# The second half of an output product in two rounds, and an expert weight load that waits on the first of them

## The reference, cut to what matters

```
for l in range(DEPTH):                       # DEPTH = 2
    m = hybrid_mixer(h, ...)                 # ends in  y @ w_o
    h = layer_norm(ALPHA * h + m, ln1)       # "ln1"
    f = grouped_moe(h, w_router, ..., w_gate[l], w_up[l], w_down[l])
    h = layer_norm(ALPHA * h + f, ln2)
...
y = gates[0]*(o_diff @ w_br[0]) + gates[1]*(o_dsa @ w_br[1]) + gates[2]*(o_fox @ w_br[2])
return y @ w_o                               # 512x1024 @ 1024x1024: the output product
...
h = silu(xb @ w_gate[e]) * (xb @ w_up[e]);  return h @ w_down[e]   # one expert
```

## Time and profile before

| | us |
|---|---|
| median of 3 runs | 2340.98 (2340.57 to 2341.06) |
| the profiled execution | 2343.16 |
| its span | 2341.5 |
| TensorE busy | 2048.9 (88%) |
| VectorE busy | 935.6 (40%) |
| ScalarE busy | 656.8 (28%) |
| GpSimd busy | 194.6 (8%) |

### The profile page before, as it was taken

One profiled execution on the slowest core, in us unless ns is written; L12 is line 12 of the kernel. 1 busy time (PEld: TensorE's weight loads), 2 busy tenths in 40 slices (PEclk: granted clock), 3 DMA queues, 4 the chain that ended last, 5 costly groups with the idle time before them and its releaser, 6 DMA issues.

```text
span 2341.5 us, 29179 instructions
## 1 busy us (share of the span) xinstructions
PE 2048.9 (88%) x9720; PEld 1185.9 (51%) x9728; DVE 935.6 (40%) x1817; ACT 656.8 (28%) x1361; POOL 194.6 (8%) x233
## 2 busy tenths in 40 slices
PE   4999999999989988788679999989999799887882
PEld 3776676577653332222257657757767333232220
DVE  5764745444561111111268566445446411110114
ACT  3444355354310100000143435445451111000000
POOL 0000001000011111111100000010000111111111
PEclk9999999999989999999879999999999899999996
DMA  5221221222479999999832113213234999999994
GB/s 174 88 89 37 72 74 71 72 72 73 198 293 407 425 425 426 425 426 425 349 114 84 62 37 108 72 37 108 73 114 174 380 425 424 425 425 426 426 425 197
DMA packets 96160, 536.18 MB, mean 229 GB/s; under 512 B 15984, under 2 KB 18800, under 8 KB 72448
## 3 DMA queue, kind: packets, MB, share of 16 engines
q1 hardware_dynamic: 83712, 511.06, 53.9%
q0 software_dynamic: 12288, 23.11, 2.6%
HBM read 528.87 MB, written 23.07 MB: 236 GB/s over the span
## 4 chain that ended last, share of the span: by engine, by line
PE 70%; DVE 9%; DMA 8%; issue 7%; ACT 2%; another core or an unknown queue 1%; POOL 1%; SPq 1%; DVEq 0%; ACTq 0%; POOLq 0%
PE ps L980 16%; PE ps L696 10%; PE ps L698 10%; PE ps L697 10%; PE ps L996 8%; PE ps L882 5%; DMA scr<-in_w_up 4%; PE ps L798 2%; DMA spare<-in_w_up 2%; PE ps L849 2%; PE ps L820 2%; PE ps L972 1%; DMA scr<-h_rows,scr 1%; DVE small L1530 1%
## 5 line engine op out<-in xcount | busy, mean ns | idle before, releaser
L1886 DVE COPY scr<-ps 128x512 f32<-128x512 f32 x66 | 45.6, 692 | 770.9 <-PE ps L972 770.9
L696 PE MATMUL ps<-hT_lo,w_hi 128*128 128x512 f32 (+1 forms) x832 | 339.1, 408 | 15.5 <-DVE w_lo L1392 7.4
L698 PE MATMUL ps<-hT_hi,w_hi 128*128 128x512 f32 (+1 forms) x832 | 327.5, 394 | 0.0
L697 PE MATMUL ps<-hT_hi,w_lo 128*128 128x512 f32 (+1 forms) x832 | 326.6, 393 | 0.0
L1110 ACT ACTIVATE scr<-ps 128x512 f32<-128x512 f32 (+3 forms) x296 | 129.8, 440 | 399.2 <-PE ps L996 305.9
L1130 ACT ACTIVATE w_hi<-ring 128x1024 fp32r<-128x1024 f32 x124 | 130.5, 1053 | 292.9 <-PE ps L698 231.0
L1392 DVE TENSOR_TENSOR w_lo<-ring,w_hi 128x1024 fp32r<-128x1024 f32 x124 | 150.7, 1216 | 132.5 <-ACT w_hi L1130 129.1
L696 PEld LDWEIGHTS ps<-hT_lo,w_hi 128*128 128x128 f32 (+1 forms) x832 | 157.1, 189 | 54.4 <-issue 8.3
L1332 ACT ACTIVATE scr<-ps 64x512 f32<-64x512 f32 x64 | 37.7, 589 | 523.7 <-PE ps L981 523.7
L698 PEld LDWEIGHTS ps<-hT_hi,w_hi 128*128 128x128 f32 (+1 forms) x832 | 156.9, 189 | 35.7
L882 PE MATMUL ps<-scr,ring 128*128 128x512 f32 x384 | 171.7, 609 | 3.4 <-ACT scr L1110 3.4
(11 more groups left out here) (245 smaller groups left out, 3212.3 us busy)
## 6 DMA issues: line engine op xcount, KB each, us to landing
ring<-in_w_down SPq DMA_DIRECT2D x32, 2048.0 KB, 48.3
ring<-in_w_in SPq DMA_DIRECT2D x30, 2048.0 KB, 7.6
xslot<-in_w_up SPq DMA_DIRECT2D x18, 2048.0 KB, 46.1
wslot<-in_w_gate SPq DMA_DIRECT2D x16, 2048.0 KB
ring<-in_w_gate SPq DMA_DIRECT2D x16, 2048.0 KB, 44.4
ring<-in_w_up SPq DMA_DIRECT2D x16, 2048.0 KB, 48.5
scr<-in_w_down SPq DMA_DIRECT2D x16, 2048.0 KB
scr<-in_w_up SPq DMA_DIRECT2D x14, 2048.0 KB
```

The source lines that it names most:

```text
L696: mm(out, a[0], b[1], start=first, stop=False)
L697: mm(out, a[1], b[0], start=False, stop=False)
L698: return mm(out, a[0], b[0], start=False, stop=last)
```

## The change

The first half of the output product is as before. The second half is done in two rounds. Round one runs over all four tiles with only the low parts of `y`, 8 matmuls each. After its last matmul a new signal, `low_used`, ticks. Round two runs over the four tiles with the two products of `y_hi`, 16 matmuls each, and marks the bank full after each tile. The transposes keep their places behind tiles 2 and 3. SyncE's wait for slot 3 (piece 6), where `y_lo` lies, is now on `low_used` instead of on `("m", 3, 1)`.

```
@@ SyncE
                         elif s == 1:
                             multiplied(("m", NT - 1, 0))
+                        elif s == MRING:
+                            sp.wait_ge(low_used.sem, low_used.at("m", l))
+                            alone(sp)
                         elif s == H_SLOT:
@@ TensorE
-                    for half in range(2):
-                        for t in range(NT):
-                            free(4 + t, l)
-                            for k in range(KD):
-                                if t == 0:
-
-                                    pe.wait_ge(wo_ready.sem, wo_ready.at((half, k), l))
-                                    alone(pe)
...
-                                ins = product(t, half, k)
-                            filled(ins, 4 + t, ("m", t, half))
-                            if half and t >= 2:
-                                transpose_tile("ln1", t - 2, l)
+                    for t in range(NT):
+                        free(4 + t, l)
+                        for k in range(KD):
...
+                            ins = product(t, 0, k)
+                        filled(ins, 4 + t, ("m", t, 0))
+                    for t in range(NT):
+                        free(4 + t, l)
+                        for k in range(KD):
+                            if t == 0:
+
+                                pe.wait_ge(wo_ready.sem, wo_ready.at((1, k), l))
+                                alone(pe)
+                            ins = mm(bank[4 + t].t, y_lo[:, k, tok(t)], wo_hi(1, k), start=(k == 0), stop=False)
+                    ins.then_inc(low_used.sem, low_used.tick("m"))
+                    for t in range(NT):
+                        for k in range(KD):
+                            mm(bank[4 + t].t, y_hi[:, k, tok(t)], wo_lo(1, k), start=False, stop=False)
+                            ins = mm(bank[4 + t].t, y_hi[:, k, tok(t)], wo_hi(1, k), start=False, stop=(k == KD - 1))
+                        filled(ins, 4 + t, ("m", t, 1))
+                        if t >= 2:
+                            transpose_tile("ln1", t - 2, l)
```

More of the change, by code:

```diff
@@ L346, in trunk @@
         wo_ready = signal("wo_ready")
+        low_used = signal("low_used")
         aff_ready = signal("aff_ready")
@@ L889, in product @@
                                              (wo_hi(half, k), wo_lo(half, k)), k == 0, k == KD - 1)
-                    for half in range(2):
-                        for t in range(NT):
-                            free(4 + t, l)
-                            for k in range(KD):
-                                if t == 0:
-                                    pe.wait_ge(wo_ready.sem, wo_ready.at((half, k), l))
-                                    alone(pe)
-                                if t == 0 and half == 0:
-                                    pe.wait_ge(y_ready.sem, y_ready.at(("y", k), l))
-                                    alone(pe)
-                                ins = product(t, half, k)
-                            filled(ins, 4 + t, ("m", t, half))
-                            if half and t >= 2:
-                                transpose_tile("ln1", t - 2, l)
+                    for t in range(NT):
+                        free(4 + t, l)
+                        for k in range(KD):
+                            if t == 0:
+                                pe.wait_ge(wo_ready.sem, wo_ready.at((0, k), l))
+                                alone(pe)
+                                pe.wait_ge(y_ready.sem, y_ready.at(("y", k), l))
+                                alone(pe)
+                            ins = product(t, 0, k)
+                        filled(ins, 4 + t, ("m", t, 0))
```

## The result

The changed kernel took 2350.15 us, the median of 6 runs (2347.53 to 2357.32), beside 2340.64 us for the kernel before. The ratio is 1.0041, with a 95% interval of 1.0030 to 1.0053: **slower by 9.5 us** (7 to 12). Forecast were +5.7 us. All runs of both kernels made in this study, 20 of the changed one and 88 of the one before, have medians of 2349.08 and 2341.17 us. So the cost is about **7.9 us**. That lies near the lower end of the first measurement's interval; the two later series of the changed kernel alone gave +7.1 and +7.2 us.

The account below looks back on a forecast made before the run. Bound by the chain leading to expert 0, not by the weight stream. Per layer 2.6 + 1.6 - 0.3 = 3.9 us; two layers 7.8 less 2.1 back: +5.7 us, 2346.7 us; range -0.6 to +8.3 us (2340.4 to 2349.3).

Parts of the forecast that it names:

- the norm queue: VectorE's layer norm after the second half: tiles arrive faster than its 5.04 us each, router product 2.6 us late per layer.
- Given back: Expert stage: earlier pieces 14 and 15 remove stream dips, returning 1.4 us in the first layer and 0.7 in the second.
- Piece 6 and the dry stream: SyncE's weight stream: piece 6 out at about 651.3 us, DMA dry from about 697 until piece 12; no gain.
- The clock: TensorE's 2.6 us gap before tile 2's transposes halves the clock around router product and sum: +1.6 us per layer.
- The gather: Expert 0's first gather: issued at 690.4 us, 0.3 us shorter per layer, its length hardly following the DMA backlog.
- The third rival: First gather short once the DMA backlog is small, 3.5 us less per layer: -1.3 us in all, the same; chance 0.10.
- the two refunds: Dips before piece 14 in the expert stage vanish: 1.4 us back in the first layer, 0.7 in the second.
- the clock's bound: Most the low clock could cost at the router product and the sum behind it: 2.3 us instead of 1.6.

Follow-up runs that it names:

- load_real: Kernel before in its old order, early load added; second half's low-`y` product replaced by repeating the low-weights product: 2341.72 us beside 2341.12, ratio 1.0001.
- order_only: Changed kernel, but the load into the low parts' buffer waits again for the second half's last product: 2350.64 us, ratio 1.0044 to the kernel before.
- gap_filled: Changed kernel plus three useless matmuls between the transposes of tiles 1 and 2: 2348.69 us, ratio 1.0032; repeated 2345.29 us, 1.0021.
- delay4: Kernel before plus five useless matmuls in front of the router's product, nothing else: 2352.90 us, ratio 1.0052.
- whole2: Changed kernel with tiles 0 and 1 of the second half kept whole, only tiles 2 and 3 in two rounds: 2340.69 us beside 2341.05, ratio 0.9999.
- before_b: Kernel before, unchanged, measured against itself and profiled again: 2342.14 us, ratio 0.9999.

## Why the prediction was wrong

The direction, the norm queue and the fall of the clock were right. The step that failed is **"Given back"**: 2.1 us were to return, and the stretches show 0.5 us, which is less than their scatter. By the prediction's own steps:

- **Piece 6 and the dry stream.** Forecast 7.6 us after the end of the first half; 7.60. DMA was forecast dry from 697, which is 693.5 on this trace's clock; it is at 123 GB/s from 694 and at 20 from 695. That the early load is worth nothing is shown best by load_real, which has the load without gain or cost; order_only has the cost without it. The rule of the Trainium skill (Perfetto Trace Analysis, section Optimization Strategy), by which mixing stages with different busy engines may improve performance, gave nothing here; two kernels fill that idle time and both keep their time.
- **The norm queue.** Forecast: first tile 11.08 us after the end of the first half, one tile each 5.04 us, a gap of 2.6 us. Measured: 11.18, 5.0 and 2.45. The selection without the clock's part is 2.65 us late (gap_filled). Right.
- **The clock.** Forecast 2.8 us for the router's product and 0.3 for the sum. Measured 2.79 in four layers of the three profiles, 2.65 and 2.58 in the other two, and the sum unchanged at 0.83 in five of the six. The prediction held that nothing would bring the clock back before the filler products; in the profile shown it is at 1.00 again from 672 to 674 us, ahead of the fillers. In the sixth layer, and in one of order_only's two, the low clock caught the transposes and the sum too and cost 1.3 to 1.4 us more. So the term is 1.4 us in most layers and 2.7 to 2.8 in some; 1.6 lies between.
- **The gather.** Issued 46.58 us after the end of the first half, forecast 46.7. Its length of 6.82 us is 0.15 under before's 6.97; 0.3 were taken. With it piece 12 is 3.88 us late, against a forecast of 3.9. The third rival had the gather short once the backlog is small. That came true for the next gathers, which were issued at 697.2 and 698.5 us into idle DMA and landed in 2.7 and 2.9 us; the first one had DMA still at some 400 GB/s beside it until 694 us.

The gather and its length stand in the chain that ended last, in the changed kernel:

```profile
686.77 6.82 DMA scr<-h_rows,scr
```

- **Given back: this is the step that failed.** The prediction let 2.1 us return, by this chain: the wait for the second gather vanishes, so TensorE comes to expert 1 sooner after expert 0, so piece 14 goes out before the stream runs low, and a dip that is gone is time won. The first link is right: the gather falls into idle DMA, and the wait of 0.95 us for its rows is gone. The second one hardly held in the first layer. TensorE's first product of expert 1 stood behind VectorE's copy of the gathered rows, and that copy stands in VectorE's queue behind the hidden values of expert 0. Of the changed kernel, VectorE's and TensorE's timelines:

```profile
703.06 0.69 DVE L1916 TENSOR_TENSOR scr<-scr,ps 64x512 f32<-64x512 f32 x1 [4.84 <-ACT scr L1348]
703.78 0.69 DVE L1902 COPY scr<-ps 128x512 f32<-128x512 f32 x1
```

```profile
704.81 0.64 PE L996 MATMUL ps<-wslot,scr 128*64 128x512 f32 x1 [1.81 <-DVE scr L1902]
```

And of the kernel before:

```profile
702.67 0.69 DVE L1900 TENSOR_TENSOR scr<-scr,ps 64x512 f32<-64x512 f32 x1 [4.84 <-ACT scr L1332]
703.62 0.69 DVE L1886 COPY scr<-ps 128x512 f32<-128x512 f32 x1 [0.26 <-PE ps L972]
```

The copy's own wait of 0.26 us is all that the faster gather could save. Piece 14 follows piece 12 after 11.27 us instead of 11.51 (713.84 - 702.57, against 713.68 - 702.17), and the stream still dips. The window of the kernel before beside the 307 GB/s of the changed one:

```profile
713.00:717.00 4.00, 3.27 (x21) 1.47 (x20) 1.72 (x3) 0.59 (x1) 0.00 (x0) 1.00 0.80 266
```

By the prediction's own measure the dip was worth 4 x (425 - 266) / 425 = 1.5 us and is worth 1.1 us now. A part of the 11.27 us is the clock. Behind the 1.81 us of idle time it fell in the first layer of the changed kernel's three profiles, and held in order_only, which has the same idle time; the second matmul of expert 1's gate product in the changed kernel, then in order_only, 0.80 and 0.43 us ahead of the next of its line:

```profile
705.28 1.01 PE L996 MATMUL ps<-wslot,scr 128*64 128x512 f32 x1
```

```profile
704.50 0.59 PE L993 MATMUL ps<-wslot,scr 128*64 128x512 f32 x1
```

Where it held, in seven of the 13 profiles, piece 14 followed piece 12 after 9.58 or 9.59 us. And there the last link can be tested, that an earlier piece 14 is time won. It is not borne out: from piece 12 to the last store of the first layer these seven take 447.6 to 449.5 us, and the six with 11.27 to 11.51 us take 447.6 to 448.4. The lead of 1.7 us is still there at piece 32 and gone at piece 52, which goes out 166.8 to 167.8 us behind piece 12 in the seven and 166.9 to 167.4 in the six. In the second layer of the changed kernel piece 14 did follow sooner, after 9.58 us instead of 10.23, and nothing came back. What takes the lead away stays open.

Behind the selection the layers take 476.48 us in the mean of the changed kernel's three profiles and 477.24 before in the first layer (0.8 us given back, less than the scatter), and 478.00 against 477.73 in the second (nothing). delay4 gives back nothing either.

So the sum is 4.0 + 4.5 us to the selection (8.5, with the toss of the clock in the second layer), less 0.5 behind it: 8.0 us, and 7.9 us is what 20 and 88 runs say. With no refund the prediction's own terms give 7.8 us. That this comes so near is in part luck, since the second layer's 4.5 us hold one toss of the clock. No step shows the 1.6 us between 7.9 and the +9.5 us of the first measurement. The spread of a median of six runs can hold them, but this is argued and not shown: the three traced executions of the changed kernel are the fastest or second fastest of their series, and what the slower ones lose was not traced. +7.9 us lies inside the range and +9.5 us lies 0.85 us above its upper end. That end allowed for one of the two refunds lost, no gain at the gather and the clock's bound, and took nothing for the spread of a six run median, although two stages hang on a clock that falls in some executions and not in others.

## What to carry to other kernels

Before a buffer is freed early, ask what the next load behind it waits for. If that is a computed event, the early load only moves the idle time of the stream to another place. Regrouping products so that results come late and close together costs where the engine behind them works in order and needs longer per tile than the new distance; half of the tiles left as they were (whole2) kept the early load at no cost. A saving behind a delay counts only if every wait on the path of the next event is followed through, the in-order queue of the engine that releases it included. And a load that goes out earlier is a gain only if its lead is still there at the end of the stage.

## What the hardware showed that was not expected

- The same idle time does not always have the same effect on TensorE's clock. Behind 1.98 us at 106 to 108 us the granted clock was 0.57 over 4 us in one execution and 1.00 in another of one program. Behind 2.45 us it fell in each of six layers, in one of them before the very next matmuls and in the others a us or two later. Behind 1.81 to 1.82 us, in front of expert 1, it fell in 4 of 11 first layers and in 1 of 11 second layers. Behind 1.04 us it held in four of four.
- A stretch of 2.74 us of matmuls without use kept the clock up: the router's product behind them was back at 1.50 us, in four of four layers.
- The first gather took 6.97 us before (6.81 in before_b), 6.82 in the changed kernel, 6.21 in order_only and 6.07 in load_real. Nothing of that follows the point at which the stream runs dry, which is 5 us earlier in the changed kernel and in load_real. In idle DMA the later gathers of the changed kernel landed in 2.7 and 2.9 us.
- The median of a few runs of this kernel moves: 2340.98 us (3 runs), then 2341.05, 2341.12 and 2341.77 (17, 22 and 31, on three chips, so that chip and chance cannot be told apart), with single runs from 2336.56 to 2346.45.
